# Sorting the small products of a chunked delta-rule loop by array shape

## What is computed

```python
def step(S, inp):
    rt, wt, kt, vt, at, bt = inp
    S = (S * wt[:, :, None, :]
         + jnp.einsum('bhij,bhj->bhi', S, at)[..., None] * bt[:, :, None, :]
         + vt[..., None] * kt[:, :, None, :])
    return S, jnp.einsum('bhij,bhj->bhi', S, rt)
...
S_fin, y = lax.scan(step, S0.astype(f32), (tm(r4), tm(w4), tm(k4), tm(v4), tm(avec), tm(bvec)))
```

## Time and profile before

| | |
|---|---|
| median of 3 runs | 4460.08 us (4458.1 to 4463.04) |
| span of the profiled execution | 4467.6 us |
| other time of that execution | none listed |
| mean granted TensorE clock | 0.930 of full |
| TensorE matmul busy | 3948.9 us, 88% |
| VectorE busy | 1918.9 us, 43% |
| chunk loop, first Gram product to last state product | 1323.6 to 1740.5 us of the span |

### The profile page before, as it was taken

The page is one execution under the profiler, slowest core; times in us unless marked ns, Lnnn a source line. Parts: engine busy times, 40 slices in busy tenths (PEclk is TensorE's granted clock), DMA queues, the critical chain, the costliest instruction groups (busy, mean ns, idle before and its releaser), DMA issues. The chain is left out here.

```text
span 4467.6 us, 73766 instructions
## 1 busy us (share of the span) xinstructions
PE 3948.9 (88%) x30029; PEld 3593.7 (80%) x30029; DVE 1918.9 (43%) x2612; ACT 1238.4 (28%) x1462; POOL 77.4 (2%) x120
## 2 busy tenths in 40 slices
PE   8989986757629998888998879999999999999998
PEld 8989975532228886778998419999999999999997
DVE  3224347758685555433232113333434334343343
ACT  3111126647613333422131202221211212122122
POOL 0000000000000000000000000000000000000000
PEclk9999988879858888999999989999999999999999
DMA  4322237759500000472222352222222222222222
GB/s 151 114 104 85 94 131 245 246 186 375 198 38 1 0 0 15 158 259 99 84 76 103 113 191 94 75 86 95 86 95 95 86 95 86 95 90 91 93 88 77
DMA packets 104474, 501.85 MB, mean 112 GB/s; under 512 B 14305, under 2 KB 20898, under 8 KB 67650
## 3 DMA queue, kind: packets, MB, share of 16 engines
q1 hardware_dynamic: 98082, 479.16, 30.1%
q0 software_dynamic: 6208, 19.93, 1.2%
HBM read 474.55 MB, written 24.50 MB: 112 GB/s over the span
## 5 line engine op out<-in xcount | busy, mean ns | idle before, releaser
L2112 PE MATMUL ps<-hf_hi,whi_f 128*128 128x260 f32 x2816 | 568.3, 283 | 19.1 <-DVE x L2102 11.1
L2112 PE MATMUL ps<-hf_hi,wlo_f 128*128 128x260 f32 x2816 | 567.9, 283 | 0.0
L2112 PE MATMUL ps<-hf_lo,whi_f 128*128 128x260 f32 x2816 | 567.0, 283 | 0.0
L182 ACT ACTIVATE whi_f<-raw 128x2048 fp32r<-128x2048 f32 x132 | 252.8, 1915 | 969.9 <-PE ps L2112 947.6
L2112 PEld LDWEIGHTS ps<-hf_hi,whi_f 128*128 128x128 f32 x2816 | 434.8, 189 | 20.9 <-DVE x L2102 14.5
L2112 PEld LDWEIGHTS ps<-hf_hi,wlo_f 128*128 128x128 f32 x2816 | 434.6, 189 | 0.0
L2112 PEld LDWEIGHTS ps<-hf_lo,whi_f 128*128 128x128 f32 x2816 | 433.6, 188 | 0.0
L186 DVE TENSOR_TENSOR wlo_f<-raw,whi_f 128x2048 fp32r<-128x2048 f32 x132 | 302.6, 2293 | 146.7 <-ACT whi_f L182 146.7
L220 PE MATMUL ps<-h_hi,whi_a 128*128 128x260 f32 x1600 | 324.2, 284 | 29.0 <-DVE h_lo L265 17.7
L220 PE MATMUL ps<-h_hi,wlo_a 128*128 128x260 f32 x1600 | 324.0, 284 | 0.0
L220 PE MATMUL ps<-h_lo,whi_a 128*128 128x260 f32 x1600 | 323.7, 284 | 0.0
(11 more groups left out here) (373 smaller groups left out, 6734.7 us busy)
## 6 DMA issues: line engine op xcount, KB each, us to landing
raw<-w SPq DMA_DIRECT2D x262, 1024.0 KB, 4.8
page_ring<-kc SPq DMA_DIRECT2D x128, 512.0 KB, 4.5
page_ring<-vc SPq DMA_DIRECT2D x64, 512.0 KB, 5.4
page_ring_more<-vc SPq DMA_DIRECT2D x64, 512.0 KB, 5.6
mem_ring<-mkc SPq DMA_DIRECT2D x8, 2048.0 KB, 8.0
mem_ring<-mvc SPq DMA_DIRECT2D x8, 2048.0 KB, 8.1
qkv<-ev_a POOLq DMA_DIRECT2D x24, 260.0 KB, 2.3
qkv_head<-qkv SPq DMA_DIRECT2D x8, 780.0 KB, 6.5
```

Source lines behind the costliest of these rows:

```text
L182: act.activation(whi[:, u, :], raw[:, u, :], ACT.Copy).then_inc(whi_done, 1)
L2112: mm = pe.matmul(ps[:, 2 * u + s, 0:m], wt[:, wslot, kcol:kcol + 128], t[:, k, a:a + m], start=(first and wt is whi and t is th), stop=(la ...
```

## The change

The Gram stage does the products of 64x128 for all four tiles and then those of 64x64 for all four tiles. The exchanged product for "d" is dropped: its result is also in the left columns of banks 2 and 3, and `powers` reads it there; the remaining 64x64 products lie side by side in banks 0 and 1. The inverse is applied with 16 products of 128x64, two column groups for each tile, with `heads`. The output stage does its 8 products of 128x128 first and then the 16 of 128x64; only the first product clears the bank's marks.

```diff
-                def blocks(t):
-                    return t.rearrange("p (a b) -> p a b", a=4)
+                def blocks(t, n=128):
+                    return t.rearrange("p (a b) -> p a b", b=n)
...
-                                src = ps[rows, 4 * q + (off > 0), :].rearrange("p (a m b) -> p a m b", a=4, m=2)[:, :, m, :]
+                                if m:
+                                    src = blocks(ps[rows, 4 * q + (off > 0), 0:256], 64)
+                                else:
+                                    src = blocks(ps[rows, 4 * q + 2 + (off > 0), :])[:, :, 0:64]
...
                         def grams(q):
                             for n in range(4):
-                                j = 4 * q + n
                                 for rows, b in ((AA, 2), (BB, 3)):
-                                    pe.matmul(ps[:, 4 * q + b, n * 128:n * 128 + 128], stg[rows, j, 2:4, :], stg[rows, j, 0:2, :],
-                                              start=True, stop=True)
+                                    pe.matmul(ps[:, 4 * q + b, n * 128:n * 128 + 128], stg[rows, 4 * q + n, 2:4, :],
+                                              stg[rows, 4 * q + n, 0:2, :], start=True, stop=True)
+                            for n in range(4):
                                 for rows, unit, b in ((AA, 2, 0), (BB, 3, 1)):
-                                    pe.matmul(ps[rows, 4 * q + b, n * 128:n * 128 + 64], stg[rows, j, unit, :], stg[rows, j, 0, :],
-                                              start=True, stop=True)
-                                    mm = pe.matmul(ps[rows, 4 * q + b, n * 128 + 64:n * 128 + 128], stg[rows, j, 0, :],
-                                                   stg[rows, j, unit, :], start=True, stop=True)
+                                    mm = pe.matmul(ps[rows, 4 * q + b, n * 64:n * 64 + 64], stg[rows, 4 * q + n, 0, :],
+                                                   stg[rows, 4 * q + n, unit, :], start=True, stop=True)
                             mm.then_inc(P0.sem, 1)
...
                             pe.wait_ge(A.sem, at(c, A, "rhs"))
-                            for j in range(RT):
-                                mm = pe.matmul(ps[:, 7, j * 64:j * 64 + 64], xs[:, j, :], rh[:, j, :], start=True, stop=True)
-                            mm.then_inc(P.sem, 1)
+                            heads(7, lambda x, j: xs[:, j, 64 * x:64 * x + 64], lambda x, j: rh[:, j, :])
                             pe.wait_ge(A.sem, at(c, A, "za"))
                             pe.wait_ge(W.sem, at(c, W, "zb"))
                             for j in range(RT):
+                                pe.matmul(ps[:, 4, j * 64:j * 64 + 64], sbd[:, j, :], rc[:, j, :], start=(j == 0), stop=False,
+                                          skip_group_check=True)
+                            for j in range(RT):
                                 js = slice(j * 64, j * 64 + 64)
-                                pe.matmul(ps[:, 4, js], sbd[:, j, :], rc[:, j, :], start=True, stop=False, skip_group_check=True)
                                 for rows, x in ((AA, 0), (BB, 1)):
                                     mm = pe.matmul(ps[rows, 4, js], zb[:, x, j, :], gr[:, x, j, :], start=False, stop=True,
                                                    skip_group_check=True)
```

## The result

The changed kernel takes 4403.06 us (median of 4 runs, 4400.16 to 4406.05), the kernel before 4460.56 (4 runs): a ratio of 0.9872, 95% interval 0.986 to 0.9884. It is 57.5 us faster; 70 were forecast, and the range was 4366 to 4414.

A forecast was written before the change was run, and what follows sets the result against it. TensorE's own queue was taken to bound the loop nearly everywhere. Savings of 12 + 22 + 16.5 + 4.7 = 55 us at half clock, or 87 at full clock; the middle, 70, gave 4460.1 - 70 = 4390 us, range 4366 to 4414.

The forecast's parts named there:

- Prices of passes and gaps: Gram and output stages: passes stream, plus a gap per change of shape; first Gram stage 1.72 us, output stage 2.9.
- The unknown: Gram stages: a 64x128 pair costs 0.112 to 0.21 us at full clock; 0.112 taken, the upper bound costs 12 us.
- The start of the output stage: Before the output stage: VectorE's copy sets its start, 1.6 us earlier per chunk, 12 us in all.
- The clock: Chunk loop: falls near the output stage in most chunks, back at about the second Gram stage; 70 us less altogether.
- as now: Rival, chunk loop: half clock over the same work as before the change; 55 us less, 4405; chance 0.17.
- full throughout: Rival, chunk loop: clock at full nearly throughout; 87 us less, 4373; chance 0.12.
- full-clock case: Rival, chunk loop: the change removes gaps, so full clock nearly throughout; 87 us less, 4373; chance 0.12.
- The wait for the other half's masks: Behind the second Gram stage: masks and identity sum end 3.6 us after it; at full clock TensorE waits 0.9.
- the gaps belong to each product: Rival, sorted stages: each new product costs a gap, not the shape; 18 us less, 4442; chance 0.02.
- the slower case: Rival: longer waits before output and second Gram stages keep half clock; up to 137 us more, 4597; chance 0.04.

## Why the prediction was right, and where not

**Prices of passes and gaps: right.** First Gram stage 1.71 us (1.72 forecast), at half clock 3.06 (3.06), output stage 2.91 at full clock (2.9). The passes of 64x64 are 256, and the loop takes 44.9 us per chunk (41 to 46). The unknown, whether pairs of 64x128 stream, fell on the lower bound: 1.10 us for eight pairs and the gap, as worked out.

**The start of the output stage: right.** It comes 4.48 us after the first Gram stage (4.4 forecast), behind a wait of 1.62 us (1.55) that goes to VectorE's copy. The inverse's new form is worth next to nothing by itself; the experiment with it alone shows that.

**The clock: rose further than forecast, and its falls were put in the wrong place.** I took the middle between "as now" and "full throughout", with the clock falling near the output stage in most chunks. It is nearly at full: nine stretches of 3.4 us behind the first Gram products, 31 us in all, where there were some 17 us per chunk. Five of the nine begin behind the wait for the sum with the identity, which I had put at 0.9 us. Each us of half clock costs about half a us where TensorE is the bound (0.112 against 0.213 per pass), so some 15 us remain of the full-clock case's gain.

**The wait for the other half's masks: the step that failed.** The prediction had VectorE beginning the masks 0.13 us after the second Gram stage, as in the earlier trace rows, 3.6 us in all and 0.9 of waiting. But in the kernel before that stage ends 5.4 us after it starts, and the state's own chain is through 2.7 us before that. With 1.71 us the chain is late instead: two sums, two decays, two copies on ScalarE (to 1502.38), the turn, then masks at 1502.99. That is 1.5 us later than forecast. Another 0.87 come from GpSimd's product beside the sum with the identity: GpSimd starts 2.9 us after the second Gram stage does in both kernels, but the sum is earlier now and meets it. From the second Gram stage to the later products it is 7.68 us and not 5.3: 2.4 x 7 = 17 us. Taking away each of the two causes gave 13.5 and 6.8 us back, about half of the first through the clock.

**The account.** Full-clock case 87 us, less 17 for this wait, less some 15 for the half clock that is left: 55, against 55.4 in the loop and 57.5 by the medians. The stages ahead of the loop's first chunk gave 3.1 us of the 4.7 forecast (15.3 us to the later products before, 12.2 now, with waits of 0.75 and 2.55 for the same sum), which makes it 53; the half-clock figure is not good enough to tell these apart. The forecast's 70 came from a clock gain that was put too small and a wait that was missing, which partly cancel. That the time lies within the range is in part luck. Of the rivals, the full-clock case was nearest in mechanism; that the gaps belong to each product is out (L1390 and L1394 stream while the product changes), and so is the slower case: its longer waits came and no stretch grew.

## What to carry to other kernels

Products of different array shapes in turn cost a gap at each change, here 0.15 to 0.20 us at full clock and as much as the small products themselves; sort them by shape before counting what a dropped product saves. When a stage of the bound engine is cut to a third, follow every other engine's program from the previous stage's end to the next wait: a step that was early by 2.7 us can be late without a line of it changed, and a wait placed only to pass on a signal is the first to take out. Where TensorE's clock is at stake, look at every empty wait in a period: filling two of three gave nothing here, and with all of them short or filled the clock stayed up.

## What the runs showed of the hardware

A change of shape between 128x128, 128x64, 64x128 and 64x64 costs 0.15 to 0.20 us at full and 0.19 to 0.30 at half clock in these traces. A 32-bit full-array pass costs 0.112 us at full clock whether 64 or 128 columns stream, and a pair of 128x64 or 64x64 passes with 64 columns 0.058, a pair of 64x128 passes 0.112. I had not expected that waits of 1.6 to 3.0 us, in a loop otherwise without gaps, would be followed once per chunk or so by 3.4 us at half clock, nor that a VectorE instruction with two SBUF inputs would take 1.56 us beside one GpSimd instruction where it takes 0.69 alone.
